# The third tile pair of two more wide passes as seven block products, and a later operand batch

## What is computed

```python
h = h + rms_norm(mixed @ w_out, mix_norm_post)
f = rms_norm(h, ffn_norm_pre)                                   # 256 x 2048
f = (silu(f @ w_gate) * (f @ w_up)) @ w_down                    # 2048 -> 5632 -> 2048
h = h + rms_norm(f, ffn_norm_post)
gate = sigmoid(rms_norm(h, ple_norm_pre) @ w_ple_gate)          # 2048 -> 2048
e = (p @ w_ple) * gate
h = h + rms_norm(e, ple_norm_post)
```

## Time and profile before

| | |
|---|---|
| median of 3 runs | 1998.52 us (1998.19 to 1999.02) |
| profiled execution | 1998.74 us |
| its span, first to last instruction | 1997.1 us |
| TensorE matmuls | busy 1984.4 us, 99%, 10149 instructions |
| VectorE | busy 1669.6 us, 84% |
| ScalarE | busy 1147.8 us, 57% |
| DMA | 394.74 MB, mean 198 GB/s |
| mean granted TensorE clock | 0.999 |

### The profile page before, as it was taken

One profiled execution on the slowest core, in us unless ns is written; L12 is line 12 of the kernel. 1 busy time (PEld: TensorE's weight loads), 2 busy tenths in 40 slices (PEclk: granted clock), 3 DMA queues, 4 the chain that ended last, 5 costly groups with the idle time before them and its releaser, 6 DMA issues.

```text
span 1997.1 us, 29428 instructions
## 1 busy us (share of the span) xinstructions
PE 1984.4 (99%) x10149; PEld 1681.8 (84%) x10149; DVE 1669.6 (84%) x2336; ACT 1147.8 (57%) x1482; POOL 18.8 (1%) x37
## 2 busy tenths in 40 slices
PE   9999999999999999999999999999999999999998
PEld 8888888888888888998888888888888888888886
DVE  7788888889888868767777787999999988888887
ACT  6666566666655545565545565556555554555575
POOL 0000000000000000000000000000000000000000
PEclk9999999999999999999999999999999999999999
DMA  8666676666566566545557667666666666766764
GB/s 233 201 190 190 190 206 183 185 198 191 169 210 209 191 200 221 155 131 161 189 189 239 202 207 241 191 201 198 191 201 199 202 198 202 252 200 205 243 190 152
DMA packets 255197, 394.74 MB, mean 198 GB/s; under 512 B 28840, under 2 KB 161440, under 8 KB 252928
## 3 DMA queue, kind: packets, MB, share of 16 engines
q1 hardware_dynamic: 251104, 369.87, 59.8%
q0 software_dynamic: 3824, 23.43, 3.6%
q10 hardware_dynamic: 176, 0.20, 0.0%
HBM read 387.08 MB, written 6.36 MB: 197 GB/s over the span
## 4 chain that ended last, share of the span: by engine, by line
PE 98%; DVE 1%; DMA 1%; ACT 0%; SPq 0%; issue 0%; DVEq 0%; ACTq 0%
PE acc L654 16%; PE acc L850 15%; PE acc L851 15%; PE acc L852 15%; PE acc L659 8%; PE acc L911 6%; PE acc L912 6%; PE acc L913 6%; PE acc L1106 1%; PE acc L784 1%; PE acc L636 1%; PE acc L635 1%; PE acc L637 1%; PE acc L1037 1%; PE acc L1241 0%; DMA raw<-w_in_in 0%
## 5 line engine op out<-in xcount | busy, mean ns | idle before, releaser
L1913 DVE TENSOR_TENSOR wlo<-raw,whi 128x1024 fp32r<-128x1024 f32 (+2 forms) x559 | 663.2, 1206 | 111.8 <-ACT whi L1350 109.4
L1350 ACT ACTIVATE whi<-raw 128x1024 fp32r<-128x1024 f32 (+1 forms) x560 | 572.3, 1044 | 248.7 <-PE acc L852 83.6
L654 PE MATMUL acc<-u,whi 128*128 128x512 f32 x1376 | 328.7, 391 | 0.0
L850 PE MATMUL acc<-whi,u 128*128 128x512 f32 x824 | 323.1, 392 | 0.1
L851 PE MATMUL acc<-wlo,u 128*128 128x512 f32 x824 | 320.8, 389 | 0.0
L852 PE MATMUL acc<-whi,u 128*128 128x512 f32 x824 | 320.8, 389 | 0.0
L654 PEld LDWEIGHTS acc<-u,whi 128*128 128x128 f32 x1376 | 252.8, 188 | 48.8
L850 PE MATMUL acc<-whi,g 128*128 128x512 f32 x520 | 203.0, 390 | 0.1
L851 PE MATMUL acc<-wlo,g 128*128 128x512 f32 x520 | 202.6, 390 | 0.0
L852 PE MATMUL acc<-whi,g 128*128 128x512 f32 x520 | 202.3, 389 | 0.0
L1373 ACT ACTIVATE whi<-raw 128x1024 fp32r<-128x1024 f32 x72 | 76.5, 1062 | 212.7 <-PE acc L913 171.7
(11 more groups left out here) (597 smaller groups left out, 2996.7 us busy)
## 6 DMA issues: line engine op xcount, KB each, us to landing
raw<-w_in_in SPq DMA_DIRECT2D x208, 512.0 KB, 3.9
raw<-w_gate_in SPq DMA_DIRECT2D x176, 256.0 KB, 2.9
raw<-w_up_in SPq DMA_DIRECT2D x176, 256.0 KB, 3.3
raw<-w_down_in SPq DMA_DIRECT2D x88, 512.0 KB, 4.7
raw<-w_ssm_o_in SPq DMA_DIRECT2D x64, 512.0 KB, 4.5
raw<-w_in_in SPq DMA_DIRECT2D x64, 256.0 KB, 4.1
raw<-w_attn_o_in SPq DMA_DIRECT2D x32, 512.0 KB, 4.7
raw<-w_out_in SPq DMA_DIRECT2D x32, 512.0 KB, 5.1
```

Source lines behind the costliest of these rows:

```text
L654: return T.matmul(bank(banks[i]), wh[:, j, i * P:i * P + P], src[:, kts[j], :, :].rearrange("p a s -> p (a s)"), start=start and j == 0, s ...
L850: T.matmul(o, x_hi, wh[:, j, :], start=start, stop=False, skip_group_check=True)
L1350: S.activation(whi[:, slot, 0:w], raw[:, slot, 0:w], ACT.Copy).then_inc(sem("hi_ready"), 1)
L1913: V.tensor_tensor(wlo[:, slot, 0:w], raw[:, slot, 0:w], whi[:, slot, 0:w].bitcast(F32), ALU.subtract) \
```

## The change

`SEVEN` for ff pass 10 and for `pg` gets pair 2 as a third seven-product pair (passes 1 to 9 of `ff` have it already), and `PAIRS["pg"]` takes the order of `ff` and `wo`, so the first such pair of `pg` is at chunk 4 instead of 6. Since pass 10 now needs the operand of pair 2 while ff pass 9's results are written to g[36:40], `xf_new2` moves from G0 + 36*2048 to E0 + 6144. That is the place of `xe` for dn pairs 2 and 3, so the batch (dn, 2, 2) is no longer built in ff pass 2 but in dn pass 0, behind chunk 19 (sums), 20 (high) and 22 (low); it now needs the additions that give the full tiles, and the down passes take pairs 2 and 3 last. `xp_new` and its buffers grow to three pairs, and the additions for `pg` become a helper, `operand_tiles`, that runs before the hidden norm. `MERGE` follows: for ff 10 chunk 14 instead of 10, for pg 14 instead of 12. The remaining lines adapt waits.

```diff
--- before.py
+++ after.py
@@ -74,29 +74,29 @@
     "pz": (8, 1),
 }
 FF_LAST = PHASES["ff"][1] - 1
-FF_THREES = (1, 2, 3, 4, 5, 6, 7, 8, 9)
 PASSES = (("so", 0), ("so", 1), ("ao", 0), ("ao", 1), ("wo", 0)) + tuple(("ff", _j) for _j in range(1, FF_LAST + 1)) \
     + (("dn", 0), ("dn", 1), ("pg", 0))
 SEVEN = {("so", _j): (0, 1, 2, 3, 4, 5, 6) for _j in range(2)}
 SEVEN.update({("ao", _j): (0, 1, 2) for _j in range(2)})
 SEVEN["wo", 0] = (0, 1, 2)
-SEVEN["pg", 0] = (0, 1)
-SEVEN.update({("ff", _j): (0, 1, 2) if _j in FF_THREES else (0, 1) for _j in range(1, FF_LAST + 1)})
-SEVEN.update({("dn", _j): (0, 1, 2, 3, 4, 5, 6, 7, 8) for _j in range(2)})
+SEVEN["pg", 0] = (0, 1, 2)
+SEVEN.update({("ff", _j): (0, 1, 2) for _j in range(1, FF_LAST + 1)})
+SEVEN.update({("dn", _j): (0, 1, 4, 5, 6, 7, 8, 2, 3) for _j in range(2)})
 PAIRS = {
     "so": (7, 8, 0, 9, 1, 10, 2, 11, 3, 12, 4, 13, 5, 14, 6, 15),
     "ao": (3, 0, 4, 1, 5, 2, 6, 7),
     "wo": (3, 4, 0, 5, 1, 6, 2, 7),
     "ff": (3, 4, 0, 5, 1, 6, 2, 7),
-    "pg": (2, 3, 4, 0, 5, 1, 6, 7),
+    "pg": (3, 4, 0, 5, 1, 6, 2, 7),
     "dn": (9, 10) + tuple(itertools.chain(*zip(SEVEN["dn", 0], range(11, 20)))) + (20, 21),
 }
 PAIRS_AT = {"so": 16, "ao": 16, "wo": 0, "ff": 0, "dn": 0, "pg": 0}
 MERGE = {_p: PAIRS_AT[_p[0]] + 2 * PAIRS[_p[0]].index(SEVEN[_p][-1]) + 2 for _p in PASSES}
 SEVENS_BEFORE = {_p: sum(len(SEVEN[_q]) for _q in PASSES[:_i]) for _i, _p in enumerate(PASSES)}
 OPERANDS = (("so", 0, 3), ("so", 3, 2), ("so", 5, 2), ("ao", 0, 3), ("wo", 0, 3), ("ff", 0, 1), ("ff", 1, 1), ("ff", 2, 1),
-            ("dn", 0, 2), ("dn", 2, 2), ("dn", 4, 2), ("dn", 6, 2), ("dn", 8, 1), ("pg", 0, 2))
+            ("dn", 0, 2), ("dn", 4, 2), ("dn", 6, 2), ("dn", 8, 1), ("dn", 2, 2), ("pg", 0, 3))
 AO_OPERANDS, WO_OPERANDS, FF_OPERANDS, DN_OPERANDS, PG_OPERANDS = 3, 4, 5, 8, 13
+DN_OPERAND_AT = {1: 0, 3: 1, 4: 2}
 WO_TILE = 16
 
 
@@ -271,15 +271,15 @@
             at("junk_g", [P, 2, 512], G0 + 10 * 2048)]
     wp = at("wp", [P, D_MODEL], U0 + 8 * 2048)
 
-    new_ops = {"pg": at("xp_new", [P, 2, 2, 4, P], G0 + 24 * 2048, F32R),
+    new_ops = {"pg": at("xp_new", [P, 3, 2, 4, P], G0 + 24 * 2048, F32R),
                "wo": at("xw_new", [P, 3, 2, 4, P], G0 + 36 * 2048, F32R),
                "so": [at("xs_new0", [P, 3, 2, 3, P], E0, F32R), at("xs_new3", [P, 2, 2, 3, P], G0 + 40 * 2048, F32R),
                       at("xs_new5", [P, 2, 2, 3, P], E0 + 9216, F32R)], "ao": at("xa_new", [P, 3, 2, 3, P], E0, F32R),
                "ff": [at("xf_new0", [P, 1, 2, 4, P], T0 + 8192, F32R), at("xf_new1", [P, 1, 2, 4, P], E0 + 12288, F32R),
-                      at("xf_new2", [P, 1, 2, 4, P], G0 + 36 * 2048, F32R)]}
-    full_x = {"pg": at("xp_full", [P, 2, 2, 2, P], G0 + 28 * 2048), "wo": at("xw_full", [P, 3, 2, 2, P], H0), "so": at("xs_full", [P, 3, 2, 2, P], G0 + 32 * 2048), "ao": at("xa_full", [P, 3, 2, 2, P], H0 + 5120),
+                      at("xf_new2", [P, 1, 2, 4, P], E0 + 6144, F32R)]}
+    full_x = {"pg": at("xp_full", [P, 3, 2, 2, P], G0 + 30 * 2048), "wo": at("xw_full", [P, 3, 2, 2, P], H0), "so": at("xs_full", [P, 3, 2, 2, P], G0 + 32 * 2048), "ao": at("xa_full", [P, 3, 2, 2, P], H0 + 5120),
               "ff": at("xf_full", [P, 1, 2, 2, P], T0 + 4096), "dn": at("xd_full", [P, 2, 2, 2, P], T0 + 4096)}
-    new_x = {"pg": at("xp_sum", [P, 2, 4, P], G0 + 30 * 2048), "wo": at("xw_sum", [P, 3, 4, P], H0 + 6144), "so": at("xs_sum", [P, 3, 3, P], H0 + 8192), "ao": at("xa_sum", [P, 3, 3, P], H0 + 11264),
+    new_x = {"pg": at("xp_sum", [P, 3, 4, P], G0 + 34 * 2048), "wo": at("xw_sum", [P, 3, 4, P], H0 + 6144), "so": at("xs_sum", [P, 3, 3, P], H0 + 8192), "ao": at("xa_sum", [P, 3, 3, P], H0 + 11264),
              "ff": at("xf_sum", [P, 1, 4, P], T0), "dn": at("xd_sum", [P, 2, 3, P], T0)}
     xe = at("xe", [P, 4, 2, 3, P], E0, F32R)
     x9 = at("x9", [P, 1, 2, 3, P], E0 + 12288, F32R)
@@ -891,7 +891,7 @@
             done = SEVENS_BEFORE[phase, it] + n
             first, last = n == 0, n == len(SEVEN[phase, it]) - 1
             slot = c % RING
-            x_new, m = operand_of(phase, n)
+            x_new, m = operand_of(phase, p if phase == "dn" else n)
             rows = (slice(0, P), slice(P, SEQ))
 
             def weights(slot, half):
@@ -1278,9 +1278,11 @@
                 if it == 0 and i == 0:
                     pe.wait_ge(sem("ff_lo"), FF_LAST)
                 if it == 0 and i == 2:
-                    pe.wait_ge(sem("x_lo"), PG_OPERANDS - 1)
-                if it == 0 and i == 18:
-                    pe.wait_ge(sem("x_lo"), PG_OPERANDS)
+                    pe.wait_ge(sem("x_lo"), DN_OPERANDS + 3)
+                if it == 0 and i == 14:
+                    pe.wait_ge(sem("x_lo"), DN_OPERANDS + 4)
+                if it == 0 and i == 16:
+                    pe.wait_ge(sem("x_lo"), DN_OPERANDS + 5)
                 if it == 1 and i == 2:
                     pe.wait_ge(sem("dn_ev"), 4)
                     pe.wait_ge(sem("dn_sq"), 4)
@@ -1325,7 +1327,7 @@
                 h_turned(1, 1 + c_)
         pe.wait_ge(sem("ee_ev"), 5)
         for c_ in range(16):
-            if c_ == 6:
+            if c_ == 4:
                 pe.wait_ge(sem("x_lo"), PG_OPERANDS + 1)
                 pe.wait_ge(sem("pg_act"), 2)
             wide_step("pg", 0, c_)
@@ -1355,7 +1357,7 @@
             act.wait_ge(sem("x_sum"), k + 1)
             if (ph, first) == ("so", 3):
                 act.wait_ge(sem("c_park"), 16)
-            if k == DN_OPERANDS + 2:
+            if (ph, first) == ("dn", 4):
                 act.wait_ge(sem("h_park"), 16)
             last = S.activation(operands(k)[:, :, 0, :, :], new_x[ph][:, 0:n, :, :], ACT.Copy)
             if ph not in KEPT:
@@ -1781,7 +1783,7 @@
             if j == 0:
                 act.wait_ge(sem("h_r"), 1)
             if j:
-                act.wait_ge(sem("x_lo"), DN_OPERANDS + min(j, 4))
+                act.wait_ge(sem("x_lo"), DN_OPERANDS + sum(k <= j for k in DN_OPERAND_AT))
                 act.wait_ge(sem("ff_prod"), j)
             for blk in range(2):
                 last = S.activation(sgate[:, blk, :], bank(c_bank("ff", j, 0, blk)), ACT.Silu, scale=st[:, 1, 3, blk:blk + 1])
@@ -1792,7 +1794,7 @@
             act.wait_ge(sem("ff_mm"), j + 1)
             both = turned(c_first("ff", j) + 2)
             last = S.activation(g[:, 4 * j:4 * j + 4, 0, :], both, ACT.Copy)
-            if j < 4:
+            if j + 1 in DN_OPERAND_AT:
                 last = S.activation(full_x["dn"][:, :, :, :, :].rearrange("p a t b s -> p (a t) (b s)"), both, ACT.Copy)
             last.then_inc(sem("ff_hi"), 1)
 
@@ -1806,8 +1808,8 @@
                 wide_high("ff", it, c_, (lambda: ff_high(it - 1)) if c_ == 4 else None)
                 if c_ == 2:
                     ff_gate(it - 1)
-                if it <= 4 and c_ == 12:
-                    operand_high(DN_OPERANDS + it - 1)
+                if it in DN_OPERAND_AT and c_ == 12:
+                    operand_high(DN_OPERANDS + DN_OPERAND_AT[it])
 
         act.wait_ge(sem("p_in"), 64)
         for it in range(2):
@@ -1815,8 +1817,8 @@
                 wide_high("dn", it, c_, (lambda: ff_high(FF_LAST)) if (it, c_) == (0, 4) else None)
                 if it == 0 and c_ == 2:
                     ff_gate(FF_LAST)
-                if it == 0 and c_ == 11:
-                    operand_high(PG_OPERANDS - 1)
+                if it == 0 and c_ in (11, 20):
+                    operand_high(DN_OPERANDS + (4 if c_ == 20 else 3))
                 if it == 1 and c_ in (2, 3):
                     post_squares("dn", 1, c_ - 2, ("dn", 0, 43), c_bank("dn", 0, c_ - 2, 0))
         post_squares("dn", 1, 3, None, c_bank("dn", 1, 1, 0), 2)
@@ -1928,20 +1930,27 @@
             ins.then_inc(sem("dve_step"), 1)
             dve.wait_ge(sem("dve_step"), steps[0])
 
+        def operand_tiles(k):
+
+            ph, first, n = OPERANDS[k]
+            if k:
+                dve.wait_ge(sem("x_lo"), k)
+            t0 = 2 * first + (WO_TILE if ph == "wo" else 0)
+            tiles = (u if ph in FROM_U else g)[:, t0:t0 + 2 * n, :, :]
+            tiles = tiles.rearrange("p (a t) l s -> p a t l s", t=2)
+            for t in range(2):
+                last = V.tensor_tensor(full_x[ph][:, 0:n, t, :, :].rearrange("p a b s -> p a (b s)"),
+                                       tiles[:, :, t, 0, :].bitcast(F32), tiles[:, :, t, 1, :].bitcast(F32), ALU.add)
+            link(last)
+
         def operand_sums(k):
 
             ph, first, n = OPERANDS[k]
             x_full, x_new = full_x[ph], new_x[ph]
             if k:
                 dve.wait_ge(sem("x_lo"), k)
-            if ph != "dn" or first == 8:
-                t0 = 2 * first + (WO_TILE if ph == "wo" else 0)
-                tiles = (u if ph in FROM_U else g)[:, t0:t0 + 2 * n, :, :]
-                tiles = tiles.rearrange("p (a t) l s -> p a t l s", t=2)
-                for t in range(2):
```

(27 more changed lines are left out.)

## The result

| | before | after |
|---|---|---|
| median, us (22 runs each) | 1998.55 | 2001.3 |
| lowest to highest | 1998.13 to 1999.15 | 2000.75 to 2002.48 |
| span of the profiled execution | 1997.1 | 1999.4 |

The ratio is 1.0014, with a 95% interval of 1.0008 to 1.002: 2.75 us slower, less than the 0.2% named as the limit. The forecast was 2000.8. What remains to be read is whether its parts were right.

What follows compares the result with a forecast made beforehand. TensorE's own stream was taken to set the time. Terms -0.68 - 0.55 + 1.14 - 0.02 + 0.89 + 1.5 gave +2.3 us, 2000.8 us for the median, 0.11% slower; range 1998.3 to 2002.2.

Steps and rivals of the forecast that it cites:

- What bounds the kernel: Whole kernel: TensorE's own stream sets the time, busy 1984.4 of 1997.1 us; every microsecond added or removed arrives at the end.
- Terms 1 and 2: Third seven-product pairs: three matmuls fewer in pg, -0.68 us; the same in ff 10 with a low operand, -0.55 us.
- Term 3: All ff passes: third operand moves to a slow low address, nine passes at 0.127 us each, +1.14 us.
- Rival (b): Address does not cause the two classes; pair or place in pass does, third sevens stay 4.76 us: 1999.5 us, chance 0.10.
- Term 4: First down pass: the operand batch at chunk 19 makes TensorE wait at the seven of chunk 20, +0.89 us.
- The second wait: Down pass, seven at chunk 24: forecast as no wait, VectorE being ready 0.35 us before TensorE arrives.
- Term 5: Operands for three pg pairs, needed at chunk 4: waits at pa 7, pg 0 and pg 4, together +1.5 us.
- What was costed at nothing: ff 10: extra block sums on VectorE and ScalarE cost nothing; losing the later merge's cover would cost 0.7 + 0.7 + 1.2 us.
- (a): VectorE's lead covers all new operand work in the down pass and pg, so no waits: 1998.4 us, chance 0.12.
- (c): VectorE doesn't catch up in the down pass; sevens at 24, 28, 32, 36 wait too: +3.6 us, 2004.4 us, chance 0.05.
- (d): New waits let TensorE's clock fall to 1.2 GHz; five pg chunks alone would cost 13.6 us: 2014 us, chance 0.01.

Runs made afterwards that it cites:

- E0: Not a run: start of an operand region in the code, byte 2,176 in the kernel before; 32 bytes higher there measured 1994.55 us, ratio 0.9982.
- the last experiment: Changed kernel with down-pass batch spread, pz fold earlier, pg work spread to remove every wait, and E0 moved up 96 bytes: 1992.66 us, ratio 0.9971.

## Why the prediction was right, and where it was not

- **What bounds the kernel**: right. Each edit arrived at the end with the size that TensorE's starts show, to some 0.3 us.
- **Terms 1 and 2, the matmuls**: right. The last pass's third seven takes 4.86 us and nothing in it waits.
- **Term 3, the place of `xf_new2`**: the size is right, the cause is wrong. 4.76 became 4.86 and 5.44 became 5.465 in all passes, as the sum had it; but it comes from E0 being 96 bytes off the rings modulo 256, not from its low bytes. The failing step is the reading "what sorts them is where the operand lies" as a region. The border of the regions happened to be the border between two alignments, and no row of before could part the two. That the size came out is luck to this extent: E0 + 6144, the new place, has the same 128 modulo 256 as E0; the same low place 96 bytes further would have cost nothing, as the last experiment shows. Rival (b) was right that the low address is no cause, and wrong in its time of 1999.5, since it had the class go with the pair.
- **The page cited there** (the Trainium skill, "TensorE: Matmul & The Clock Gate", LDWEIGHTS (loading the stationary operand)) gives a weight load's time by its columns and names no address. The load's duration is the same in both classes, as by that rule, though its figure for 128 columns would be 0.107 us and the rows have 0.19. Taken for the step of whole matmuls the rule would have set this term to zero; the runs show 0.2267 and 0.2342 us for one form, by addresses alone.
- **Term 4, the down pass**: right in place, cause and size: 0.81 and 0.06 us measured, 0.89 forecast. The second wait, which the sum excluded by 0.35 us, is there with hundredths: the block of chunk 24 started 10.28 us behind that of chunk 20 (1719.76) instead of the 9.97 of the sum, and 0.24 of the difference is VectorE's wait for a high part from ScalarE (1716.28).
- **Term 5, pg**: right; 0.23, 0.53 and 0.65 us for 0.30, 0.55 and 0.67. VectorE's pieces came at the distances of the chain, to a hundredth, but all of them 0.97 us later than it put them: 1921.03, 1924.30 and 1932.76 instead of 1920.06, 1923.33 and 1931.79. The chain's clock times were those of before, and by then the whole stream ran 1.0 us later, TensorE's too, so the waits came out as forecast.
- **What was costed at nothing**: here the prediction failed. I looked at the later merge of ff 10 and named its cover, and did not do the same for pg, whose merge moved from chunk 13 to chunk 15. Behind it stand pz's low parts, folds and gates, 1.2 us late, in a phase where VectorE has no lead: +0.52 us. This one term accounts for the distance between the sum's +2.3 and the measured +2.75. That it lies in the pg part is shown by undoing that part, and that the fold's place decides by moving the fold.
- **Rivals (a), (c), (d)**: the waits came, so (a) falls. Nothing behind chunk 24 waited, so (c) falls. The granted clock reads 1.00, the 2.4 GHz level, in the stretches around all these waits, the longest of 0.67 us, so (d) falls.

## What to carry to other kernels

A matmul removed is worth its step only where the helper engine has idle time for the new operand's work. Find that idle time in its timeline, compare it with the work in microseconds, and split the work over several such gaps before giving up the saving. When an edit moves a merge, follow it into the next phase at every place where it moves, not at one. And when two speeds of one instruction are sorted by address, sort them by the address modulo a small power of two as well, and against the partner operand, before speaking of a region.
